# One expert slot loaded ahead of two others in the mixture-of-experts loop of a four-layer diffusion trunk

## The reference

```
def moe_ffn(h, router, w_gu, w_down):
    top_v, top_i = lax.top_k((h @ router).astype(jnp.float32), TOP_K)
    ...                                  # combine: softmax weight of each token's two experts, 0 elsewhere
    gu = jnp.einsum('btd,edf->btef', h, w_gu)          # w_gu: (8, 1024, 2 * 1408)
    g, u = jnp.split(gu, 2, axis=-1)
    act = jax.nn.silu(g) * u * combine[..., None]
    return jnp.einsum('btef,efd->btd', act, w_down)    # w_down: (8, 1408, 1024)
```

## Time and profile before

| | us |
|---|---|
| three executions | 2337.91, 2341.35, 2343.45 |
| their median | 2341.35 |
| the profiled execution | 2342.44 |
| its span, first to last instruction | 2340.6 |
| PE busy in it | 2231.0 (95%) |
| DVE busy | 482.0 (21%) |
| ACT busy | 391.8 (17%) |

### The profile page before, as it was taken

How to read it: one execution, slowest core, us unless ns; L and a number is a source line. 1 busy time by engine, 2 the same in 40 slices (tenths; PEclk the granted TensorE clock), 3 DMA queues, 4 the chain that set the end, 5 groups by cost and what they waited for, 6 DMA issues and landing times.

```text
span 2340.6 us, 44306 instructions
## 1 busy us (share of the span) xinstructions
PE 2231.0 (95%) x19787; PEld 1662.4 (71%) x19787; DVE 482.0 (21%) x1352; ACT 391.8 (17%) x795; POOL 67.1 (3%) x109
## 2 busy tenths in 40 slices
PE   6999998999999999999998999999998989999998
PEld 4776666888888756646676588888878867466465
DVE  2334432000111400000212320002344423000002
ACT  1133223100110100000113220002143331000001
POOL 3000001000000000000000000000000000000000
PEclk8999999999999999999999899999999999999999
DMA  8967889753346499999774696413440047999992
GB/s 328 272 240 289 300 314 274 226 156 107 125 144 215 143 376 386 384 380 378 283 233 170 228 276 182 136 37 111 141 144 7 12 145 251 383 387 381 380 382 113
DMA packets 355911, 550.93 MB, mean 235 GB/s; under 512 B 11280, under 2 KB 311184, under 8 KB 343232
## 3 DMA queue, kind: packets, MB, share of 16 engines
q1 hardware_dynamic: 344352, 525.31, 64.7%
q0 software_dynamic: 5840, 18.11, 3.0%
q10 hardware_dynamic: 5536, 4.73, 0.6%
HBM read 537.64 MB, written 14.93 MB: 236 GB/s over the span
## 4 chain that ended last, share of the span: by engine, by line
PE 78%; SPq 10%; DVE 5%; ACT 2%; DMA 2%; issue 2%; ACTq 0%; DVEq 0%
PE ps L643 76%; SPq L483 7%; SPq L487 3%; ACT ring L1445 2%; DMA ring<-in_moe_w_down 1%; DVE ring L1997 1%; ACT work L1445 1%; DVE ring L2015 0%; DVE work L1856 0%; DVE ring L2020 0%; DVE ring L2005 0%; DMA ring<-in_ada_w 0%; PE ps L1141 0%; PE ps L1034 0%; DVE ring L2023 0%
## 5 line engine op out<-in xcount | busy, mean ns | idle before, releaser
L643 PE MATMUL ps<-hT,ring 128*128 128x256 f32 x3200 | 714.0, 382 | 3.4 <-DVE hT L1866 3.2
L643 PE MATMUL ps<-ring,work 128*32 128x384 f32 (+7 forms) x8008 | 692.0, 436 | 22.4 <-DMA ring<-in_moe_w_gu 5.4
L643 PEld LDWEIGHTS ps<-hT,ring 128*128 128x128 f32 x3200 | 609.0, 191 | 113.1 <-issue 12.2
L643 PEld LDWEIGHTS ps<-ring,work 128*32 128x32 f32 (+2 forms) x8008 | 390.9, 114 | 302.2 <-issue 178.6
L1445 ACT ACTIVATE work<-ps 128x256 f32<-128x256 f32 (+6 forms) x220 | 100.7, 468 | 1331.4 <-PE ps L643 1152.4
L643 PE MATMUL ps<-work,ring 128*128 128x256 f32 (+1 forms) x1344 | 288.0, 374 | 10.6 <-DVE work L2082 6.0
L643 PEld LDWEIGHTS ps<-work,ring 128*128 128x128 f32 (+1 forms) x1344 | 241.7, 187 | 46.4 <-DVE work L2082 7.7
L643 PEld LDWEIGHTS ps<-ring 64*64 64x64 f32 x4192 | 160.5, 139 | 59.3 <-ACT ring L1445 24.2
L643 PE MATMUL ps<-ring 64*64 64x64 f32 (+1 forms) x4192 | 182.7, 230 | 19.8 <-ACT ring L1445 7.2
L1445 ACT ACTIVATE ring<-ps 128x512 f32<-128x512 f32 (+3 forms) x208 | 101.7, 492 | 341.4 <-PE ps L643 330.4
L643 PE MATMUL ps<-work 128*128 128x128 f32 (+2 forms) x736 | 107.4, 297 | 4.7 <-DVE work L2202 4.6
(11 more groups left out here) (260 smaller groups left out, 933.6 us busy)
## 6 DMA issues: line engine op xcount, KB each, us to landing
ring<-in_moe_w_gu SPq DMA_DIRECT2D x96, 1536.0 KB, 16.0
ring<-in_ada_w SPq DMA_DIRECT2D x96, 1024.0 KB, 7.0
ring<-in_moe_w_down SPq DMA_DIRECT2D x48, 1536.0 KB, 16.4
ring<-in_ff_w_gu SPq DMA_DIRECT2D x88, 512.0 KB, 6.1
ring<-in_dn_w_in SPq DMA_DIRECT2D x32, 1024.0 KB, 5.6
ring<-in_moe_w_gu SPq DMA_DIRECT2D x32, 1024.0 KB, 9.1
ring<-in_ff_w_down SPq DMA_DIRECT2D x44, 512.0 KB, 7.2
ring<-in_moe_w_down SPq DMA_DIRECT2D x32, 512.0 KB, 11.6
```

The source lines that it names most:

```text
L643: return pe.matmul(out, lhsT, rhs, start=start, stop=stop, **kw)
```

## The change

The order in which one pass of SP's loop goes through the slots is changed: slot 6 (third gate columns) stands ahead of slots 2 and 3 (fourth gate and up columns with a down block each), where it stood behind them. The waits of each slot, what is loaded and where to, and the other engines' programs stay.

```
@@ -516,7 +516,7 @@
                     n_more = sp.snap(n_last + (NARROW - 1))
                     with sp.Fori(0, n_more) as r:
                         e = sp.value_load(order_e[0:1, bass.ds(r + 1, 1)], min_val=0, max_val=NE - 1)
-                        for j in (0, 1, 4, 5, 2, 3, 6, 7, 8, 9, 10):
+                        for j in (0, 1, 4, 5, 6, 2, 3, 7, 8, 9, 10):
                             if j in GU_FREE:
                                 sp.wait_ge(moe["p_gu"], (done[0] + r) * 6 + GU_FREE[j])
                                 if j == GATE_D:
```

## The result

| | before | after |
|---|---|---|
| median of 22 executions, us | 2343.22 | 2348.56 |
| lowest to highest | 2337.91 to 2347.36 | 2341.34 to 2356.75 |
| ratio, 95% interval | | 1.0026 (1.0017 to 1.0035) |
| profiled execution | 2342.44 | 2341.34 |

The change makes the kernel slower by 5.3 us, 0.26%. The forecast was 2.25 us faster, no change that can be told; the time lies outside its range of 2333.5 to 2344.0.

A forecast was written before the change was run, and what follows sets the result against it. Expert layers were taken as PE-bound first, then DMA-bound. Gains of A - 3.65 and A - 2.3, together 2A - 5.95 = 2.25 us with A = 4.1, gave 2340.2 profiled, 2339.1 against the median; range 2333.5 to 2344.0.

The forecast's parts named there:

- What bounds it: Both expert layers begin PE-bound and end DMA-bound, with SP's DMA issues blocked by a full queue.
- the hole: DMA stream gap in each layer's first expert round: 6.5 us (6.3 in layer 3), which slot 6, issued at 812.4, partly fills.
- Does A last: At the second expert's round, 4.8 us of queued work against 4.1 keeps the lead for 200 us, by 0.7 us.
- A: The DMA stream's lead from moving slot 6 into the first round's gap: one slot, 4.1 us in each layer.
- step (c): Layer 1's four DMA waits: sixth expert's two go, seventh waits 4.1 us for slot 2, last wait's 0.45 us is gained.
- The price of the order: Slots 2 and 3 come one slot later, +4.1 us, which costs in 96-token experts; slot 2 lands when it does now.
- The rule weighed there: DMA completion is not first in, first out, so slot 2's 4.1 us delay might not be paid in full.
- the first rival: Slot 2 hardly late behind slot 6; PE keeps 4.1 us per layer, 8.2 us faster, 2333.2 against the median; chance 0.15.
- 2A - 5.95: Gain of both layers together, A - 3.65 in layer 1 plus A - 2.3 in layer 3: 2.25 us.
- the second rival: Lead not gained or lost, late slot 2 paid in the seventh expert; up to 5.95 us slower, 2347.3; chance 0.12.
- Order in the 64-token experts: Slots 6 and 2 are needed together there, so the new order helps; sixth expert's 2.88 us third-columns wait goes.
- step (d): Fifth expert's second gate columns: slot 2 keeps its landing at 964.6, needed at 967.7, with 3 us to spare.

The follow-up runs named there:

- e3: Kernel before with the new order in pass 5 alone, the pass that loads the seventh expert; +12.5 us vs before, ratio 1.0045.
- e2: Changed kernel with slot 6 ahead in passes 0 to 4 only, old order from pass 5; -6.0 us vs before, ratio 0.9976.
- e4: Changed kernel with 24 unused matmuls added in the seventh expert ahead of the wait for slot 2; +4.1 us vs before, ratio 1.0021.
- e7: Changed kernel with slot 6 ahead in passes 0, 2 and 4 only, old order elsewhere; -5.9 us vs before, ratio 0.9975.
- e1: The changed kernel run again with no edit; +5.1 us vs before, ratio 1.0024.
- e8: Changed kernel with slot 4 also ahead of slot 1 in passes 1, 3 and 5; +3.9 us vs before, ratio 1.0025.
- e9: Kernel before, old order, with columns of slots 2 and 3 issued before their down block's wait; -0.3 us vs before, ratio 1.0001.

## Why the prediction was wrong

**What bounds it, and the hole: right.** The later part of the expert stages is set by the DMA stream, the hole was filled with exactly one slot (309 GB/s against 308), and slot 6 was issued at 813.3, 26.7 us into the stage (the 812.4 forecast lie at 26.9).

**Does A last: wrong, the first step that failed.** "Enough, by 0.7 us" was read from the landings of two loads, 11.5 and 6.7 us. It asked when the queue would be empty, and the rate sags before that (298 GB/s against 410). The lead was lost at the load of slot 0, ahead of slot 1, which was not asked about; but the same measure would have passed it too, with 12.5 - 6.7 = 5.8 us against 4.1. So it is the measure that failed, and not only the choice of the load. Of 1.5 MB, 1.0 to 1.2 MB lasted, 2.6 to 3.0 us at 383 GB/s. For slot 2 of the seventh expert the lead, from e3 against after, was 276.82 - 274.37 = 2.45 us and 276.95 - 275.01 = 1.94 us, not 4.1; e2 against before gives 2.23 and 1.96. Why this is some 0.6 us less than the bytes say stays open. For the same reason a wait stayed that step (c) had go: PE waited 1.25 and 1.68 us before the down projection of the sixth expert.

**The price of the order: right in kind, small in size.** 4.3 and 4.8 us against 4.1. The rule weighed there, that completion is not first in, first out, would have made it less, and did not; the first rival fell with it.

**The sum.** Its own formula, 2A - 5.95, with the leads 2.45 and 1.94 (their sum is 2A) gives -1.6 us, a small loss: the second rival, which had 0.12. The form of the sum was right, the value of A was not, and with the prices of 4.3 and 4.8 us it turns at A = 3.4 even without the clock. Between the forecast (-2.25) and what the stages show (+4.5) lie 6.8 us: 3.8 of them are the lead, 0.8 the price, 3.3 the clock, and 1.2 go the other way (the wait for ACT below, and what the rows don't hold). I had listed the loss of the lead as a rival and priced it, then taken a margin of 0.7 us, built on two rows, for enough.

**What no step had: the clock.** The working put a wait of 4.1 us where there had been 0.53, and counted only its length. PE at 1.2 GHz after it costs 1.9 and 1.4 us more in the rows of after. The profile of before could have told. The four DMA waits of its expert stages, 2.88 us at most, had caused no fall, but a wait of 4.06 us for DVE, some 50 us ahead of the first expert stage, had. PE in order of time, then the windows of that wait and of the work behind it:

```profile
732.51 1.90 PE L643 MATMUL ps<-work,ring 128*128 128x256 f32 x4 [4.06 <-DVE work L2101]
```

```profile
728.50:732.50 4.00, 0.00 (x0) 0.00 (x0) 3.76 (x8) 0.00 (x0) 0.00 (x0) 1.00 0.71 207
732.50:736.50 4.00, 3.99 (x11) 3.23 (x12) 0.00 (x0) 0.00 (x0) 0.00 (x0) 0.57 0.51 186
```

A new wait of 4.1 us was of that length.

Term by term for the profiled execution, layer 1 and layer 3: slot 2 late +1.81 and +2.83, clock +1.92 and +1.39, last wait of before gone -0.45 and -1.79, shorter wait for ACT ahead of the 128-token expert -0.47 and -0.32; together +2.81 and +2.11, where the stages grew by 2.61 and 1.91.

**Order in the 64-token experts: right. The fifth expert: right by less than it says.** The third columns' wait is gone everywhere the new order feeds a 64-token expert. In the fifth expert after has no wait, but slot 2 does not keep its time, as step (d) has it: it lands 1.9 and 2.8 us later than in before, and of the 3 us to spare 1.2 and 0.4 are left. In e4, with the same loads, PE waited 1.00 us there in layer 3.

**Scatter.** The 22 executions of after spread over 15.4 us, those of before over 9.5, and the longer ones have the lower mean clock: 0.974 at 2356.7, 0.981 at 2341.3. Part of that is seen: a shorter wait brings the clock down in one execution and not in another (last section). What moves it outside the expert stages was not tried and stays open, as does the part of e3's +12.5 that its stages (+10.1) don't hold.

The better version is e7 or e2. In e7 slot 6 goes ahead only where a 64-token expert uses slots 6 and 2 together, and wherever a 96-token expert needs slot 2 before slot 6 the old order stays; e2 keeps it for the last of these alone. Both beat both kernels, e2 with 2337.25 us against 2343.24 of before, e7 with 2337.63 against 2343.56. They can't be told apart by their times, but e7 leaves the fifth expert 4.7 us to spare and e2 0.6 to 0.8.

## What to carry to other kernels

Order the loads of a stream by the order in which the consumer of that very round needs them; one order for rounds of two kinds pays in the one and costs in the other, and the round that decides is the one in which the engine catches up with the stream. A lead in a stream is worth only what the next wait for a free buffer lets through: sum the bytes of the windows and look for the place where it shrinks. And price a wait that gets longer by what TensorE does after it as well as by its length.

## What the runs showed of the hardware

All eight waits of 3.45 to 5.2 us on PE that the study's profiles hold ahead of the seventh expert's second gate columns (two each in after, e1, e3 and e8) brought the clock to 0.50, and the 160 records behind them took 11.95 to 13.40 us in place of 10.61. Ahead of the expert stages a wait of 4.06 us for DVE did so in all thirteen profiles. Shorter waits do it in one execution and not in another: a wait of 3.1 us for DVE behind the first stage in ten of the thirteen. The 2.88 and 2.54 us of before did not, nor did three of the four such waits in e3 and e9; the fourth, of 2.66 us, did, and so did one of 1.99 us in e8, alone among the twenty waits of 1.1 to 2.0 us before the sixth expert's down projection. PE in order of time, e9 (64 records in 7.05 us, 5.35 otherwise), then e8 (48 records, 5.36 otherwise):

```profile
2185.41 7.05 PE L646 MATMUL ps<-ring,work 128*32 128x384 f32 x64 [2.66 <-DMA ring<-in_moe_w_gu]
```

```profile
1032.04 7.05 PE L652 MATMUL ps<-ring,work 128*32 128x512 f32 x48 [1.99 <-DMA ring<-in_moe_w_down]
...
1061.67 13.40 PE L652 MATMUL ps<-ring,work 128*32 128x384 f32 x160 [3.45 <-DMA ring<-in_moe_w_down]
```

So the waits of 2.5 to 2.9 us that e2 removes carry such a chance as well, which one profile of before can't show. And with few loads left in the queue the DMA rate sags while they are still under way: 298 GB/s in e1 against 410 in before, over the two microseconds from 58 us of the stage on.
